# A hybrid decoder step on one core: eight dummy products in the router chain taken out

## The chip, the cores and the metric

The kernel runs on one core of one Trainium2 chip. The metric is device time in microseconds (us) of one execution. A core has five engines that run side by side and meet through semaphores: TensorE (PE, the matrix engine, whose weight loads are listed apart as PEld), VectorE (DVE), ScalarE (ACT), GpSimd (POOL) and SyncE (SP, which here only issues DMA transfers). TensorE's clock is granted at 2.4 GHz (1.00 in the profile) or at half of that (0.50).

## The reference: what is computed

One decoder layer over 264 tokens (256 of a prompt and 8 samples), all float32, model width 1024:

```
x += W_out( sigmoid(Ga h) * HGRN2(h) + sigmoid(Gb h) * MultiScalePool(h) ),  h = RMSNorm(x)
x += MoE_top4of32_clampedSwiGLU(RMSNorm(x))
x += sigmoid(RMSNorm(x) W_pg) * (p_i W_pp)
```

and a last RMSNorm. The part that matters here is the second line. A router (1024 x 32) gives each token 32 logits; the best four experts are picked, and their softmax weighs them. Each of the 32 experts has three 1024 x 1024 weight matrices (gate, up, down), some 403 MB together:

```
gate = min(xb @ w_gate[e] + b_gate[e], 7);  up = clip(xb @ w_up[e] + b_up[e], -7, 7)
act  = (up + 1) * gate * sigmoid(1.702 * gate);  y = act @ w_down[e] + b_down[e]
```

## The kernel before, in words

Every engine has one instruction stream, written out by hand in order. There is no planner: an engine does its instructions one after another and waits where `wait_ge` says so.

**Up to the router.** Projections, the recurrent mixer, the pooling mixer and W_out are computed for three token tiles (128, 128 and 8 tokens). PSUM banks are handed out by a fixed list of jobs; `fill_done` tells that TensorE has filled a bank, `drain_done` that VectorE ("v") or ScalarE ("a") has emptied it.

**The router chain** (lines 858 to 883 on TensorE, 1502 to 1566 on VectorE):
- TensorE turns the normalised rows h2 (line 587) and multiplies them by the router matrix (`logits`, line 854), tile by tile; tile 1 is the last.
- VectorE adds the bias, finds the best values and their indices (lines 1506 to 1519), makes a one-hot of them (line 1525) and the mask `msk` of chosen experts (line 1526). That last instruction raises semaphore `s_rt` to 2.
- TensorE meanwhile runs six dummy products (`keep_warm(6, bank[5])`, line 868, recorded under line 597): 128x128 identity by 128x256 of h2, into a bank that nobody reads. It then waits for `s_rt` 2 and computes the *rank* of each token within its expert (lines 873 and 876: products of a triangular matrix or ones with `msk`) and the *count* per expert (line 882). Then come two more dummies (line 884).
- VectorE turns the ranks into slot numbers (lines 1534 and 1540) and makes the first token selector `oh` (`select_tokens(0)`, line 1489).

**Between the router and the loop.** TensorE gathers the tokens of the first two experts (`gather`, line 926, and `gather_samples`, line 936), with `turn_weights` (line 892) and the bias products `down_biases` (lines 904 and 909) in between. VectorE builds the routing tables all this while, then adds the bias products to x (lines 1470 and 1572) and signals the banks free. ScalarE copies the gathered rows to SBUF (`rows_in`, line 1212).

**The expert loop** runs 16 times, each time over a pair of experts: bias products (line 986), gate and up and down products (line 970), the next pair's gather (926, 936), transposes (944, 1000), and the combination back to tokens (1010, 1014). The weights come as granules of 1 MB, 24 per pair, into a ring of 16 places. SP issues the load of granule n at line 414 once `s_used` has reached n + 1. The first 16 loads are let go by instructions far ahead of the loop (the last of them by the turning of h2), so the ring is full before the loop starts. Load 17 is let go by the product with the first granule in the loop, and so on, one load for one granule used.

**After the loop** come the per-layer-input gate (weights loaded by the same queue, line 422 and 424) and the last norm.

Gate and up products read their selector, their rows and the banks as these waits say:

```
pe.wait_ge(s_esel, i + 1)
pe.wait_ge(s_xe, 2 * i + 1)
pe.wait_ge(s_free23, i + 1)
```

Of the kernel before, what the change touches and what calls it, by code (L numbers as in the profile page):

```python
# [126 lines left out]
def build(nc, x_prompt, x_sample, p_prompt, p_sample, state_hgrn, state_pool, g_mix, w_in,  # L127
          hg_lb_logits, hg_norm, w_pool, pool_scale, w_out, g_ffn, w_router, b_router, w_gate, b_gate,
          w_up, b_up, w_down, b_down, g_ple, w_ple_gate, w_ple_proj, g_final,
          y_prompt, y_sample, new_hgrn_prompt, new_pool_prompt, new_hgrn_sample, new_pool_sample):  # L130
    jobs = bank_jobs()
    order = {name: n for n, (name, _, _) in enumerate(jobs)}
    drainer = {name: e for name, _, e in jobs}
    drain_count, before = {}, {}
    seen, last = {"a": 0, "v": 0}, {}
# [6 lines left out]
    with ExitStack() as ctx:  # L142
# [4 lines left out]
        bank = [ctx.enter_context(nc.psum_tensor(f"bank{n}", [P, HALF], F32)) for n in range(8)]  # L147
        at = [0]

        def take(floats):  # L150
            at[0] += floats
            assert at[0] <= 53200, at[0]
            return at[0] - floats

        def view(start, floats, rows=P):
            return arena[0:rows, start:start + floats]
# [11 lines left out]
        ident = view(take(P), P)  # L168
# [23 lines left out]
        def rows3(start):  # L192
            return view(start, 3 * D).rearrange("p (t d) -> p t d", t=3)
# [33 lines left out]
        h2 = rows3(OG)  # L227
# [105 lines left out]
        def fill_done(ins, name):  # L333
            ins.then_inc(filled, 1)
# [29 lines left out]
        def piece(name):  # L364
            _, t, n = name
            return job_bank(name)[:, :] if t < 2 else job_bank(name)[32 * n:32 * n + NS, 0:256]
# [204 lines left out]
        def _(pe):  # L571
# [19 lines left out]
                                ins.then_inc(s_used, 1)  # L591
                        fill_done(ins, name)

            def keep_warm(n, out):

                for _ in range(n):
                    pe.matmul(out[:, 0:256], ident, h2[:, 0, 0:256], start=True, stop=True)

            def wait_turned(tag, tiles=range(NT)):
                for t in tiles:  # L600
                    for half in range(2 if t < 2 else 1):
                        wait_drained(pe, (tag, t, half))
# [50 lines left out]
            for kind in ("f", "q"):  # L653
                for h in range(H):
# [3 lines left out]
                    for k in range(KD):  # L658
                        ins = pe.matmul(job_bank((kind, h))[:, 0:T],  # L659
                                        w_slot[c % NSLOT][:, k, (h % 4) * P:(h % 4 + 1) * P], hT[:, k, :],  # L660
                                        start=(k == 0), stop=(k == KD - 1))
# [8 lines left out]
            for a in range(2):  # L670
                for b in range(NS):
                    for j in range(4):
                        h = 2 * j + a
                        pe.matmul(bank[7][32 * j:32 * j + NS, a * P:(a + 1) * P], qm[:, h, b, :], s0[:, b, h, :],
                                  start=(b == 0), stop=(b == NS - 1))
            for h in range(H):
                ins = pe.matmul(bank[7][0:NS, 2 * P + h:2 * P + h + 1], qk_s[:, h, :], ones[:, 0:1],
                                start=True, stop=True)
# [20 lines left out]
            for t in range(2):  # L699
                for half in range(2):  # L700
                    name = ("score", t, half)
                    begin(name)
                    for j in range(4):
                        h = 4 * half + j
                        ins = pe.matmul(job_bank(name)[:, j * P:(j + 1) * P], t1[:, h, toks(t)], qh[:, h, toks(t)],
                                        start=True, stop=True)
# [36 lines left out]
            for t in range(2):  # L743
                for half in range(2):
# [3 lines left out]
                    for j in range(4):  # L748
# [3 lines left out]
                                  start=(j == 0), stop=True, skip_group_check=True)  # L752
                    wait_drained(pe, ("dS", t, half, 3))
                    for j in range(4):
                        h = 4 * half + j
                        for c in range(4):
                            n = 4 * t + c
# [29 lines left out]
            for k in range(2):  # L787
                for g in range(4):
                    ins = pe.matmul(piece(("yp", 2, g)), dT[:, 2 * g + k, toks(2)], wpool[:, g, k, :],
                                    start=(k == 0), stop=(k == 1))  # L790
                    if k == 1:
                        fill_done(ins, ("yp", 2, g))
            for t in range(2):
                for half in range(2):
                    name = ("yp", t, half)
                    begin(name)
                    for gg in range(2):
                        g = 2 * half + gg
                        for k in range(2):
                            ins = pe.matmul(job_bank(name)[lanes(t), gg * 256:(gg + 1) * 256],  # L800
                                            dT[:, 2 * g + k, toks(t)], wpool[:, g, k, :],
                                            start=(k == 0), stop=(k == 1))
# [62 lines left out]
            wait_turned("h2T", (1,))  # L865
            fill_done(logits(1), ("lg",))

            keep_warm(6, bank[5])
            pe.wait_ge(s_rt, 2)
            begin(("rank",))  # L870
            for t in range(NT):
# [8 lines left out]
            for t in range(NT):  # L880
                n = TS[t]
                ins = pe.matmul(bank[2][0:8, 0:NE], ones[0:n, 0:8], msk[0:n, t, :], start=(t == 0), stop=(t == NT - 1))
            fill_done(ins, ("count",))
            keep_warm(2, bank[5])

            def turn_weights():

                pe.wait_ge(s_rt, 3)
                begin(("wT",))
                for t in range(NT):  # L890
                    for r in range(4):
                        ins = pe.matmul(bank[3][r * NE:(r + 1) * NE, toks(t)], wdn[lanes(t), t, :],
                                        ident[lanes(t), lanes(t)], start=True, stop=True, tile_position=(0, r * NE))
                fill_done(ins, ("wT",))
# [770 lines left out]
```

## Time and profile before

| what | value |
|---|---|
| time, three runs | 1355.17, 1355.27 and 1357.8 us, median 1355.27 |
| the profiled execution's own time | 1357.17 us |
| its span in the trace | 1355.4 us |
| PE busy | 1253.1 us (92%) |
| PEld, DVE, ACT, POOL busy | 575.4, 334.2, 185.3, 66.7 us |
| mean granted TensorE clock | 0.988 |
| moved by DMA | 458.72 MB, mean 338 GB/s |

The span is from the first to the last recorded instruction; the time of the execution has 1.8 us more around it. PE's busy time includes products at either clock level and products whose result nobody uses. An engine's busy share says little about the end; what a stage is worth is read from the waits and the chain of that stage.

### The profile page before, as it was taken

The numbers are of one execution on the slowest core, as the hardware profiler recorded it, in microseconds if no ns is written. First come the engines' busy times: TensorE is split into PE (matmuls) and PEld (weight loads), VectorE is DVE, ScalarE is ACT, GpSimd is POOL, SyncE is SP. The second block draws the span as 40 slices with busy tenths as digits, with TensorE's granted clock in tenths as the row PEclk, the third lists the DMA queues.
The fourth block names the chain that finished last, engine by engine and source line by source line (L and its number), as shares of the span: only waits on it lengthen the run. The fifth ranks groups of instructions, "written<-read, shape, count | busy, mean of one in ns | idle before, by whom it ended". The sixth has DMA issues, their size and how long they took to land.

```text
span 1355.4 us, 15937 instructions
## 1 busy us (share of the span) xinstructions
PE 1253.1 (92%) x6319; PEld 575.4 (42%) x6319; DVE 334.2 (25%) x635; ACT 185.3 (14%) x359; POOL 66.7 (5%) x142
## 2 busy tenths in 40 slices
PE   6999999899999999999998999999898999999895
PEld 5764445365543433434333343433334343333342
DVE  2423335132422212122111212211121221112123
ACT  3313312212001001000000100000010000001042
POOL 7020110130000000000000000000000000000000
PEclk9999999999899999999999999999999999999988
DMA  9734251575499999999999999999999999999920
GB/s 330 257 112 155 84 216 64 188 273 189 162 423 422 421 422 422 422 422 422 422 422 422 422 422 422 422 422 422 423 422 422 422 422 422 422 422 422 419 84 32
DMA packets 79360, 458.72 MB, mean 338 GB/s; under 512 B 8553, under 2 KB 9729, under 8 KB 30176
## 3 DMA queue, kind: packets, MB, share of 16 engines
q1 hardware_dynamic: 73936, 444.66, 80.2%
q0 software_dynamic: 3888, 12.88, 3.2%
q10 hardware_dynamic: 1504, 0.75, 0.2%
q8 instruction: 21, 0.34, 0.1%
q14 instruction: 11, 0.09, 0.0%
HBM read 452.36 MB, written 6.35 MB: 338 GB/s over the span
## 4 chain that ended last, share of the span: by engine, by line
PE 68%; DMA 26%; DVE 3%; ACT 1%; issue 1%; SPq 1%; POOL 0%; DVEq 0%; ACTq 0%
PE bank L970 32%; DMA arena<-in_w_down_dram 22%; PE bank L618 10%; PE bank L821 5%; PE bank L1010 4%; PE bank L659 3%; PE bank L926 3%; DMA arena<-in_w_up_dram 2%; DMA arena<-in_w_ple_proj_dram 1%; PE bank L641 1%; PE bank L936 1%; PE bank L986 1%; PE bank L1014 1%; PE bank L587 1%; PE bank L828 1%
## 5 line engine op out<-in xcount | busy, mean ns | idle before, releaser
L970 PE MATMUL bank<-arena 128*64 128x512 f32 x3072 | 677.1, 594 | 48.0 <-DMA arena<-in_w_up_dram 31.5
L970 PEld LDWEIGHTS bank<-arena 128*64 128x64 f32 x3072 | 229.3, 137 | 480.6 <-issue 480.3
L618 PE MATMUL bank<-arena 128*128 128x512 f32 x320 | 145.5, 609 | 4.5 <-ACT arena L1060 3.0
L618 PEld LDWEIGHTS bank<-arena 128*128 128x128 f32 x320 | 60.5, 194 | 81.1 <-issue 77.7
L1607 DVE TENSOR_TENSOR arena<-bank,arena 128x512 f32<-128x512 f32 (+1 forms) x96 | 61.5, 683 | 78.0 <-PE bank L1010 77.8
L926 PEld LDWEIGHTS bank<-arena 128*128 128x128 f32 x544 | 66.7, 196 | 27.2 <-issue 27.2
L926 PE MATMUL bank<-arena 128*128 128x128 f32 x544 | 73.4, 288 | 0.0
L1591 DVE TENSOR_SCALAR arena<-bank 128x512 f32<-128x512 f32 x32 | 20.6, 687 | 200.1 <-PE bank L970 200.1
L1601 DVE COPY arena<-bank 128x512 f32<-128x512 f32 x16 | 11.1, 692 | 235.8 <-PE bank L970 235.8
L821 PE MATMUL bank<-arena 128*128 128x512 f32 x144 | 65.5, 615 | 3.2 <-issue 3.2
L1585 DVE TENSOR_SCALAR arena<-bank 128x512 f32<-128x512 f32 x32 | 20.6, 687 | 186.4 <-PE bank L970 186.4
L659 PE MATMUL bank<-arena 128*128 128x264 f32 x256 | 60.9, 403 | 3.2 <-DVE arena L1333 2.6
L1010 PE MATMUL bank<-arena 128*128 128x512 f32 x128 | 59.2, 605 | 0.0
L1221 ACT ACTIVATE arena<-arena 128x1024 f32<-128x1024 f32 x16 | 16.9, 1058 | 293.0 <-DVE arena L1585 293.0
L659 PEld LDWEIGHTS bank<-arena 128*128 128x128 f32 x256 | 50.8, 199 | 12.9 <-issue 3.0
L461 POOL DMA_DIRECT2D out_dram<-arena x3 | 1.7, 551 | 1047.2 <-DVE arena L1639 1047.2
L1223 ACT ACTIVATE arena<-bank 128x264 f32<-128x264 f32 x16 | 6.3, 392 | 289.1 <-PE bank L1000 289.1
L821 PEld LDWEIGHTS bank<-arena 128*128 128x128 f32 x144 | 28.1, 198 | 38.4 <-issue 38.3
L1225 ACT ACTIVATE arena<-bank 128x512 f32<-128x512 f32 x16 | 9.6, 598 | 236.5 <-PE bank L970 236.5
L1010 PEld LDWEIGHTS bank<-arena 128*128 128x128 f32 x128 | 23.0, 189 | 24.9 <-issue 23.0
L1269 DVE COPY arena<-bank 128x512 f32<-128x512 f32 (+3 forms) x22 | 12.3, 569 | 76.7 <-PE bank L781 42.4
L944 PE MATMUL bank<-arena 128*128 128x128 f32 x128 | 19.6, 296 | 10.3 <-DVE arena L1596 10.3
(230 smaller groups left out, 730.1 us busy)
## 6 DMA issues: line engine op xcount, KB each, us to landing
arena<-in_w_gate_dram SPq DMA_DIRECT2D x128, 1024.0 KB, 26.3
arena<-in_w_up_dram SPq DMA_DIRECT2D x128, 1024.0 KB, 26.4
arena<-in_w_down_dram SPq DMA_DIRECT2D x128, 1024.0 KB, 26.3
arena<-in_w_in_dram SPq DMA_DIRECT2D x14, 2048.0 KB, 12.1
out_dram<-arena POOLq DMA_DIRECT2D x11, 512.0 KB, 3.8
arena<-in_state_hgrn_dram POOLq DMA_DIRECT2D x8, 512.0 KB, 14.2
arena<-in_w_out_dram SPq DMA_DIRECT2D x4, 1024.0 KB, 8.1
arena<-in_w_ple_gate_dram SPq DMA_DIRECT2D x4, 1024.0 KB, 26.7
```

The lines of the kernel that those rows point to most:

```text
L587: ins = pe.transpose(job_bank(name)[:, j * n:(j + 1) * n], src[0:n, t, k * P:(k + 1) * P], ident[0:n, 0:n])
L618: ins = pe.matmul(job_bank(name)[:, :], hT[:, k, toks(t)], w[:, k, :], start=(k == 0), stop=(k == KD - 1))
L659: ins = pe.matmul(job_bank((kind, h))[:, 0:T], w_slot[c % NSLOT][:, k, (h % 4) * P:(h % 4 + 1) * P], hT[:, k, :], start=(k == 0), stop=(k ...
L821: ins = pe.matmul(job_bank(name)[:, :], src[:, k, toks(t)], weights(w, k, half), start=(k == 0), stop=(k == slices - 1))
L926: ins = pe.matmul(XG[k // 4][:, (k % 4) * P:(k % 4 + 1) * P], h2[:, t, every_other(k)], oh[:, t, :], start=(k % 4 == 0 and t == 0), stop=F ...
L944: ins = pe.transpose(out[c][:, j * P:(j + 1) * P], src[:, every_other(k)], ident)
L970: ins = pe.matmul(out[c][hp(one), :], src[:, k * P + CAP * one:k * P + CAP * one + CAP], w[one][:, j, halves(c)], start=(first and k == 0) ...
L1010: ins = pe.matmul(banks[c][:, :], comb[:, toks(t)], y_sb[:, halves(c)], start=True, stop=True)
L1221: act.activation(sig_sb, g_sb, ACT.Sigmoid, scale=ALPHA).then_inc(s_gsig, 1)
L1585: ins = dve.tensor_scalar(g_sb[:, halves(c)], bank[c][:, :], LIMIT, None, ALU.min)
L1591: ins = dve.tensor_scalar(u_sb[:, halves(c)], bank[2 + c][:, :], LIMIT, -LIMIT, ALU.min, ALU.max)
L1607: ins = dve.tensor_tensor(xs, src, xs, ALU.add)
```

## The change: the eight dummies are taken out

```diff
-            def keep_warm(n, out):
-
-                for _ in range(n):
-                    pe.matmul(out[:, 0:256], ident, h2[:, 0, 0:256], start=True, stop=True)
-
@@ TensorE, after the logits of tile 1
             fill_done(logits(1), ("lg",))
 
-            keep_warm(6, bank[5])
             pe.wait_ge(s_rt, 2)
             begin(("rank",))
@@ TensorE, after the counts
             fill_done(ins, ("count",))
-            keep_warm(2, bank[5])
-
             def turn_weights():
```

The six dummies ahead of the ranks and the two ahead of the first gather go. No wait, no transfer and no other product is changed, on any engine.

## Rows read from the trace of the kernel before

**Rows 1.** The page, 40 slices: DMA share in tenths, and GB/s.
```profile
DMA  9734251575499999999999999999999999999920
GB/s 330 257 112 155 84 216 64 188 273 189 162 423 422 421 422 422 422 422 422 422 422 422 422 422 422 422 422 422 423 422 422 422 422 422 422 422 422 419 84 32
```

**Rows 2.** DMA issues on SP: start, us, queue, line, transfer, count.
```profile
302.33 31.83 SPq L414 DMA_DIRECT2D arena<-in_w_up_dram  x8
362.77 11.49 SPq L414 DMA_DIRECT2D arena<-in_w_down_dram  x8
```

**Rows 3.** Waits of PE in the loop: total us, times, longest.
```profile
PE bank L970 <- DMA arena<-in_w_up_dram: 31.5, 24, 1.3
```

**Rows 4.** The chain that ended last, near the loop's end.
```profile
1273.78 20.23 DMA arena<-in_w_ple_proj_dram
1294.01 2.02 issue
```

**Rows 5.** The chain from the router to the loop: start, us, what, how many.
```profile
334.28 1.94 PE bank L854 x16
...
338.00 2.61 PE bank L854 x16
340.61 5.28 PE bank L597 x12
345.89 0.21 PE bank L876 x2
...
347.15 0.36 PE bank L882 x6
347.51 1.06 PE bank L597 x4
348.58 2.11 PE bank L926 x16
...
355.74 1.19 PE bank L936 x16
356.94 0.04 issue
356.98 0.61 ACT arena L1212
357.58 0.44 issue
358.02 1.14 PE bank L986 x8
```

**Rows 6.** Stretches: length, busy us of PE, PEld, DVE, ACT, POOL, PEclk, DMA, GB/s.
```profile
66.00:69.40 3.40, 3.40 (x10) 2.58 (x9) 0.25 (x1) 0.00 (x0) 0.00 (x0) 0.50 1.05 405
120.60:124.00 3.40, 3.40 (x5) 1.35 (x4) 1.03 (x4) 3.40 (x13) 0.93 (x1) 0.50 0.19 60
335.60:339.00 3.40, 2.53 (x24) 2.32 (x23) 0.80 (x2) 0.60 (x1) 0.00 (x0) 1.00 1.02 419
340.60:345.90 5.30, 5.30 (x15) 4.22 (x14) 3.14 (x17) 0.21 (x1) 0.00 (x0) 0.50 0.55 230
345.90:348.60 2.70, 2.70 (x25) 2.07 (x24) 1.29 (x5) 0.00 (x0) 0.00 (x0) 1.00 0.00 0
348.60:357.00 8.40, 8.28 (x84) 5.89 (x84) 8.04 (x24) 0.42 (x2) 0.00 (x0) 1.00 0.01 2
362.80:1290.00 927.20, 868.90 (x4304) 357.14 (x4301) 188.26 (x280) 70.02 (x96) 0.00 (x0) 1.00 1.01 421
1294.90:1301.60 6.70, 5.56 (x7) 2.50 (x8) 4.20 (x7) 4.71 (x10) 0.00 (x0) 0.50 0.04 17
```

**Rows 7.** VectorE in order of time: start, us, line, operation, [idle before].
```profile
343.17 0.81 DVE L1526 TENSOR_REDUCE arena<-arena 128x96 f32<-128x384 f32 x1
...
347.20 0.26 DVE L1534 SCALAR_TENSOR_TENSOR arena<-bank,arena 128x96 f32<-128x96 f32 x1 [3.09 <-PE bank L876]
...
347.75 0.56 DVE L1489 TENSOR_TENSOR arena<-arena 128x384 f32<-128x384 f32 x1
...
356.06 1.27 DVE L1572 TENSOR_TENSOR arena<-bank,arena 8x512 f32<-8x512 f32 x2
```

## The prediction

> **What bounds the kernel now.** I read the 40 slices of the page first. The reader is to see that from slice 12 on the DMA row stays at 9 and the traffic at 422 GB/s almost to the end, and that before it both jump about [rows 1]. The long part is therefore a steady stream of weights. The stretch table confirms it: over the 927 us from 362.8 on, the DMA engines are busy throughout (1.01) at 421 GB/s [rows 6]. TensorE is the one that waits in it: 24 waits for up granules alone, 31.5 us together [rows 3]. The chain that ended last leaves the loop through the transfer of w_ple_proj [rows 4], the tail of the same queue. So the end is the moment at which this stream starts, plus a fixed amount.
>
> The issues on SP say when it starts. Eight loads are issued in the 32 us after 302.33, and the next one comes at 362.77 [rows 2]. The ring of 16 granules is full before then, and the next load is let go when the first granule has been used. The first product of the loop, line 986, starts at 358.02 and takes 1.14 us [rows 5]; the first use ends 362.77 - 358.02 = 4.75 us after that start. So each microsecond by which the loop starts later, or by which these 4.75 us get longer, is a microsecond at the end, and the reverse. What I have to find is the new start of the loop.
>
> Third, the chain of waits from the router to the loop [rows 5], with the granted clock of its stretches [rows 6] and VectorE's instructions [rows 7]. Two facts decide. The clock is already at 0.50 when the dummies begin at 340.61, after the thin logits products (0.50 from about 339.1, since 335.6 to 339.0 is still at 1.00); it returns to 1.00 at 345.9, after 5.3 us filled by dummies without a gap. And the mask is ready at 343.17 + 0.81 = 343.98 [rows 7], but the ranks start at 345.89, because the six dummies, at half clock, are still running.
>
> **The change part by part.**
>
> *Six dummies ahead of the ranks.* Twelve records take 5.28 us, 0.44 us each. Of these 343.98 - 340.61 = 3.4 us lie beside VectorE's search for the best four; the rest, 345.89 - 344.03 = 1.86 us, is on the path. Without them the ranks start at about 344.03 (0.05 us for the semaphore, such as the 0.04 us at 356.94 [rows 5]).
>
> *The clock under the ranks.* Here the saving is paid for. Without dummies TensorE stands idle from 340.61 to 344.03, while its clock is at half. Nothing gives it back before the ranks. The ranks took 347.15 - 345.89 = 1.26 us at the full clock. How much longer is a product at half? The dummies themselves show both levels: 0.44 us a record in the row of twelve, 1.06/4 = 0.265 in the row of four, a factor of 1.66; the clocks' own ratio is 2. I take 2, because short rows of a few records carry a start and an end in them that make the ratio look smaller, and keep 1.66 as the other end. The ranks then end at 344.03 + 2.52 = 346.55 (346.1 at 1.66), 0.6 us before the old 347.15. So 1.86 us saved become 0.6.
>
> *Two dummies ahead of the gather.* The selector is ready at 347.75 + 0.56 = 348.31 [rows 7], the gather starts at 348.58 when the dummies end. They cost TensorE at most 0.27 us, and I count that as gained on TensorE's side: the gather can start 348.31 + 0.04 - 347.15 = 1.20 us after the end of the ranks.
>
> *Two chains to the loop.* VectorE's has no TensorE clock in it: from the end of the ranks it works almost without a gap (8.04 of 8.40 us from 348.6 to 357.0 [rows 6]), until its last bias additions end at 356.06 + 1.27 = 357.33 [rows 7], and the loop starts 0.69 us later. From end of ranks to loop that is 358.02 - 347.15 = 10.87 us. New: 346.55 + 10.87 = 357.42, 0.6 us earlier than before. TensorE's own: the work from the first gather to the last sample product is 356.94 - 348.58 = 8.36 us at full clock, then 0.04 and 0.61 us for ScalarE's copy and 0.04 to start. Before, it would have let the loop start at 357.62; the loop started at 358.02, so TensorE's chain had 0.4 us of slack and VectorE's was the later. (The page puts the last wait down to ScalarE, which was done 0.44 us earlier; the additions and the entry into the loop behind them fit better.)
>
> Now TensorE's chain starts at 346.55 + 1.20 = 347.75, at half clock. When does the full clock come back? Rows of before give three lengths. The stretches at 66 and at 120.6 were dense at once and lasted some 3.4 us; the dummies had it back 5.3 us after their first product; the stretch from 1294.9 lasted 6.7 us, of which TensorE was busy 5.56 [rows 6]. The gathers follow an idle place, as the dummies followed thin products, so I take 5.3: full clock at 353.05. In these 5.3 us TensorE does 2.65 us of its 8.36; the other 5.71 us end at 358.76, and the loop starts 0.69 us later, at 359.45. That is 1.43 us later than before. By the other rows: with 3.4 us at half, 347.75 + 3.4 + (8.36 - 1.7) = 357.81, loop at 358.50, +0.5; with 6.7 us, 347.75 + 6.7 + (8.36 - 3.35) = 359.46, loop at 360.15, +2.1. With the factor of 1.66 and 5.3 us (ranks end 346.1, gather from 347.3): 347.3 + 5.3 + (8.36 - 3.19) = 357.8, loop at 358.5, +0.5. The value taken is +1.4, with +0.5 and +2.1 around it. What is late next is thus TensorE's own gathers and bias products, not VectorE.
>
> *The first granule.* The 4.75 us from the loop's start to the first refill stay, if the clock is back by then. If not, they double: +4.75.
>
> *The rest.* Sixteen matmul records and their weight loads less on an engine that waits for DMA through the loop; bank 5 is read by nobody then. Nothing from that, in either direction: the 5.28 us and 1.06 us of TensorE time are on no other chain.
>
> *The sum.* -1.86 (ranks earlier) + 1.26 (ranks at half clock) gives -0.6 for the end of the ranks; -0.22 at the gather's start (348.58 to 348.35); +2.65 (half of 5.3 us lost in the gathers); -0.40 because TensorE's chain had slack. Together +1.43 us. The profiled execution, at 1357.17 us of its own (span 1355.4 and 1.8 around it), would become 1358.6. It lies 1.9 us above the median of the runs, 1355.27, and one of the three runs does too (1357.8); the difference is as large as what I am after. I put the sum on the median: 1355.27 + 1.43 = 1356.7.
>
> *A rule of the skill against this change.* In an execution in which the clock had stayed full through the logits, they would end about 0.7 us earlier, and six dummies of 0.53 us each would be done before the mask: they would then cost nothing. The trace shows no such execution. The Trainium skill (TensorE: Matmul & The Clock Gate, Why this matters for your kernels) says that idle gaps between bursts of products send the clock back to half, and its Part 1 adds that how many products run at half varies between runs of the same kernel. By that rule the new idle place of 3.4 us would itself bring a fall in such executions, and the loss would be the half-clock share of the gathers without the 1.86 us in return. No run here shows it yet; the stated spread of the three runs, 2.6 us, is at least as large as such an effect. It is priced as a rival below.
>
> **The rivals.**
>
> *A: the forecast.* The clock comes back in the middle of the gathers and bias products; +0.5 to +2.1, so 1355.8 to 1357.4, likeliest 1356.7. Chance 0.5.
>
> *B: the idle place itself brings a fall that was not there before.* An execution with full clock before would have no saving at the ranks; half clock through 5.3 us of gathers costs 2.65 less the slack of 0.4, less the 0.22 at the gather: +2.0, and with 6.7 us at half +2.7. Time 1357.3 to 1358.0. For it: stretches at half elsewhere begin after idle or thin places. Against it: in the one trace the fall came before the dummies, so this place did not need an idle TensorE. Chance 0.2.
>
> *C: clearly slower, the clock stays at half into the loop.* The mechanism is the same, the place the first granule. From 347.75 all 8.36 us take 16.72: 364.47, loop at 365.16, +7.1, and the 4.75 us of the first granule double: +11.9 in all, 1367.2. It decides from the point at which the half clock outlasts the gathers, that is over 10 us of nearly unbroken products, more than any stretch in the trace (6.7). A partial form of it, a second fall at the 1 us gap ahead of the loop (356.94 to 358.02), would cost up to 4.75 on top of the +1.4: 1361.4. Chance 0.07.
>
> *D: faster, the ranks' earlier start survives.* If the clock is back when the gathers start, or if thin products lose little at half clock, VectorE's chain decides: -0.6 with the ranks at half, -1.86 if they too ran at full. 1353.4 to 1354.7. For it: VectorE's chain was the later one, and it does not slow down. Against it: from 340.6 to 347.8 TensorE is idle or in thin products, and in the trace the clock came back only behind dummies. Chance 0.13.
>
> *E: the change reaches the end in no measurable form.* The start of the stream is shifted but the end is not, because something later than the stream sets it. Time 1355.3. Against it: 927 us without a break in the stream, and the chain through its last transfer. Chance 0.1.
>
> **How the numbers follow.** A measurement of this kernel can tell about 0.2%, 2.7 us, from no change: 1352.6 and 1358.0 are the bounds. A, D and E lie within them, B at the upper one, C above it. The median itself can fall into either group of execution times (1355.2 or 1357.5), which carries some of A and B over the upper bound. Slower: 0.07 of C, 0.06 of A and B, 0.13 together. Faster: 0.03, from the bottom of D. No measurable change: 0.84. The range from 1354.4 to 1359.2 leaves out C and the lower part of D, and holds the jump of the median between its two groups on top of A.
>
> **What would show it.** Line 597 is gone. The ranks (line 876) start about 3.4 us after the last logits product, at 344.0 if the clock falls where it fell. The granted clock is at 0.50 from before the ranks to about 353. The gather (line 926) of 16 records takes about 4 us in place of 2.11. The first product of line 986 starts at 359 to 360, and SP's first issue behind the ring comes 4.75 us later. The loop's traffic stays at 421 GB/s. The prediction is wrong if line 986 starts before 358.0, if the gathers run at 1.00, or if the start of the stream and the end move by different amounts.

## The result

| | before | after |
|---|---|---|
| median of 20 executions each | 1355.81 us | 1359.38 us |
| lowest, highest | 1352.79, 1358.34 | 1355.31, 1360.99 |
| ratio after to before | | 1.0024 (95% interval 1.0015 to 1.0033) |
| profiled execution, own time | 1357.17 | 1360.33 |
| its span | 1355.4 | 1358.6 |

The kernel without the dummies is slower by 0.24%, some 3.3 us, just over the bound of 0.2%. The two profiled executions differ by 3.2 us as well, so their traces can be compared term by term (both executions lie above their medians, by 1.4 and 1.0 us). Line numbers of after are lower: 849 is 854 of before, 870 and 867 are 876 and 873 (ranks), 918 and 928 are 926 and 936 (gathers), 978 and 962 are 986 and 970.

**Profile after.** First the chain of waits from the router to the loop (start, us, what, how many), which answers to [rows 5]:

```profile
337.89 2.65 PE bank L849 x16
...
343.08 0.81 DVE arena L1518
343.89 0.04 issue
343.94 0.64 PE bank L870 x2
...
346.28 0.23 PE bank L870 x4
...
347.90 3.75 PE bank L918 x16
...
357.15 1.19 PE bank L928 x16
358.33 0.04 issue
358.38 0.61 ACT arena L1204
358.98 0.41 issue
359.39 2.09 PE bank L978 x8
```

The reader is to see three things. The ranks start at 343.94, 0.05 us behind the mask, where before they started at 345.89. They take 346.51 - 343.94 = 2.57 us for 1.26. The first 16 records of the gather take 3.75 us for 2.11. All of the time won ahead of the ranks is lost again by 357, and 1.37 us more: the loop starts at 359.39, not 358.02.

The same stretches with the granted clock (columns as in [rows 6]):

```profile
340.60:343.90 3.30, 0.00 (x0) 0.00 (x0) 3.07 (x16) 0.21 (x1) 0.00 (x0) 0.50 0.82 345
343.90:347.90 4.00, 3.06 (x20) 2.65 (x21) 1.32 (x6) 0.00 (x0) 0.00 (x0) 0.50 0.01 4
347.90:352.60 4.70, 4.70 (x33) 4.06 (x33) 4.44 (x18) 0.00 (x0) 0.00 (x0) 0.50 0.01 3
352.80:359.30 6.50, 5.49 (x50) 3.44 (x44) 3.96 (x11) 1.31 (x3) 0.00 (x0) 1.00 0.00 0
359.60:362.90 3.30, 3.30 (x12) 0.84 (x14) 0.72 (x2) 1.16 (x1) 0.00 (x0) 0.51 0.00 0
363.10:1290.00 926.90, 868.67 (x4298) 355.83 (x4294) 188.18 (x280) 68.24 (x93) 0.00 (x0) 1.00 1.01 420
```

The clock falls before the place of the dummies, as before, but stays at half until 352.6. It is at full for 6.8 us and then falls a second time, just as the loop begins (359.4 to 362.8). In before it stayed at full from 345.9 through the whole loop [rows 6]. This second fall makes the bias products of line 978 take 2.09 us for 1.14. SP's first load behind the ring is accordingly late (start, us, queue, line, transfer; [rows 2]):

```profile
365.78 11.49 SPq L414 DMA_DIRECT2D arena<-in_w_down_dram  x8
```

That is 365.78 - 359.39 = 6.39 us behind the loop's start, against 4.75. From there on the two kernels are the same: the stream runs at 420 GB/s without a break, TensorE waits for it as long as before ([rows 3]),

```profile
PE bank L962 <- DMA arena<-in_w_up_dram: 31.4, 24, 1.3
```

and the span ends 1358.6 - 365.78 = 992.8 us behind the first refill, against 1355.4 - 362.77 = 992.6. So the 3.2 us are 1.37 (loop starts later) and 1.64 (first granule takes longer), with 0.2 left over.

VectorE's last piece of work ahead of the loop is the adding of the bias products to x, four instructions and then two. These are its lines of before and, below them, of after:

```profile
353.67 2.49 DVE L1470 TENSOR_TENSOR arena<-bank,arena 128x512 f32<-128x512 f32 x4
```

```profile
355.07 2.48 DVE L1462 TENSOR_TENSOR arena<-bank,arena 128x512 f32<-128x512 f32 x4 [2.15 <-PE bank L896]
357.47 1.27 DVE L1564 TENSOR_TENSOR arena<-bank,arena 8x512 f32<-8x512 f32 x2
```

In after VectorE stands idle for 2.15 us until TensorE's bias products (line 896) end. In before it starts the same additions at 353.67, when those products have just ended (line 904, 352.58 + 1.07 = 353.65). From the start of the bias products to the loop's first product both kernels need the same: 358.02 - 352.58 = 5.44 us and 359.39 - 353.98 = 5.41 us. The whole 1.37 us therefore arise ahead of the bias products.

### The profile page after: what moved, and what is told of

Same layout as the page of the kernel before. It is cut to its first block, busy times and chain, and to the rows that moved or that the text cites. A ratio compares the mean times of both kernels' runs of the same rounds, so it can differ in the third digit from the quotient of the medians.

```text
span 1358.6 us, 15905 instructions
## 1 busy us (share of the span) xinstructions
PE 1252.0 (92%) x6303; PEld 573.5 (42%) x6303; DVE 334.2 (25%) x635; ACT 185.0 (14%) x359; POOL 66.5 (5%) x142
## 4 chain that ended last, share of the span: by engine, by line
PE 68%; DMA 25%; DVE 3%; ACT 1%; issue 1%; SPq 1%; POOL 0%; DVEq 0%; ACTq 0%
PE bank L962 32%; DMA arena<-in_w_down_dram 22%; PE bank L613 10%; PE bank L816 5%; PE bank L1002 4%; PE bank L654 3%; PE bank L918 3%; DMA arena<-in_w_up_dram 2%; DMA arena<-in_w_ple_proj_dram 1%; PE bank L636 1%; PE bank L928 1%; PE bank L978 1%; PE bank L1006 1%; PE bank L587 1%; SPq L414 1%
```

## The experiments

Each was timed in five rounds beside the kernel before, on the same chip. Executions of one kernel spread by 2 to 8 us here, so the intervals are wide (0.1%, 1.4 us). The profiles are therefore read beside them. Where the work ahead of the router ends also moves from one execution to the next, so I give two lengths for each profile: from the end of the last logits product to the loop's first product, and on to the first refill. Half clock is what the trace grants between the logits and the first granule. A length belongs to the one execution that was profiled, and the ratio to all of them: in the twelve experiments the profiled execution lay 0.4 to 2.4 us below the kernel's median, except the first of the variant with the place ahead of the loop filled, which lay 2.2 above.

| kernel | ratio (interval) | logits to loop | loop to refill | half clock, us of the span |
|---|---|---|---|---|
| before (profiled) | 1 | 17.4 | 4.75 | 339.1 to 345.9 |
| after | 1.0024 (1.0015 to 1.0033) | 18.9 | 6.4 | 338.9 to 352.6, 359.4 to 362.8 |
| after, again | 1.0035 (1.0023 to 1.0048) | 19.0 | 6.4 | 339.3 to 352.9, 359.7 to 363.1 |
| only the six out | 1.0020 (1.0010 to 1.0030) | 18.1 | 6.45 | 338.0 to 348.2, 358.5 to 361.9 |
| only the two out | 1.0006 (0.9995 to 1.0017) | 18.8 | 6.3 | 337.8 to 344.7, 348.1 to 351.5, 358.3 to 361.7 |
| three in place of six | 1.0022 (1.0011 to 1.0034) | 19.4 | 6.2 | 338.4 to 352.1, 358.9 to 362.3 |
| twelve thin ones in place of six | 1.0016 (1.0005 to 1.0028) | 19.7 | 4.7 | 336.8 to 350.5 |
| after, place ahead of the loop filled | 0.9997 (0.9989 to 1.0006) | 19.2 | 4.7 | 339.4 to 353.1 |
| the same, again | 1.0005 (0.9993 to 1.0017) | 19.2 | 4.7 | 337.1 to 350.7 |
| before, that place filled | 0.9992 (0.9981 to 1.0004) | 16.4 | 4.7 | 337.3 to 340.7 |
| before, logits filled | 0.9990 (0.9979 to 1.0002) | 17.1 | 4.7 | 345.4 to 348.8 |
| before, ahead of and behind the loop filled | 0.9990 (0.9982 to 0.9999) | 16.5 | 4.7 | 337.9 to 341.4 |
| before, all three filled | 0.9991 (0.9982 to 1.0000) | 17.4 | 4.7 | 343.5 to 346.9 |
| all three filled, the eight out | 1.0011 (1.0001 to 1.0021) | 19.7 | 4.7 | 341.1 to 351.3 |

**Only the six out.**

```diff
-            keep_warm(6, bank[5])
```

> Only the six dummies ahead of the ranks go; the two ahead of the first gather stay. Clock theory (the loss is half-clock work: +1.4 us until the loop starts, +1.6 us in the first granule): the ranks start at 344.0 at half clock, the two dummies run at half clock (some 1.8 us instead of 1.06) and hold the gather back until about 348.6; the clock comes back no later than with all eight out (352.7), so the loop starts at 358.5 to 360. Time +1 to +4 us against the kernel before, close to the kernel after. Rival (the two dummies ahead of the gather were what kept the clock up, the six only cost): the time is that of the kernel before or 0.6 to 1.9 us less, with the loop at 356.2 to 357.4.

Measured: 1.0020, about what the whole change costs. The rival is out: the two dummies alone don't bring the time back. They do run at half clock (2.01 us for four records). The clock is back 9.2 us behind the logits, where the kernel after needed 12.1, and the loop starts 0.8 us sooner behind them. The second fall comes all the same.

**Only the two out.**

```diff
-            keep_warm(2, bank[5])
```

> Only the two dummies ahead of the first gather go; the six stay. Clock theory: the clock is back at 345.9 as before, the gather starts 0.2 to 0.3 us earlier, and VectorE's chain (10.87 us from the end of the ranks to the loop) hides that: the loop starts at 358.0, time within 0.5 us of the kernel before. Rival (the idle place of about 1 us behind the counts brings a fall): half clock in the gathers, +1.5 to +3 us.

Measured: 1.0006, an interval that takes in both no change and 0.17%. The profiled execution speaks for the rival, though: with the clock back at 344.7, TensorE idles behind the counts, and the clock falls again as the gathers begin (length, busy us by engine, PEclk, DMA, GB/s):

```profile
344.80:348.00 3.20, 2.14 (x25) 1.89 (x24) 1.74 (x7) 0.00 (x0) 0.00 (x0) 1.00 0.00 0
348.20:351.40 3.20, 3.20 (x28) 2.82 (x27) 3.01 (x13) 0.00 (x0) 0.00 (x0) 0.50 0.02 5
```

TensorE is busy for 2.14 of 3.20 us, and thinly, then at half for the gathers. In this execution the missing two cost 1.4 us up to the loop. How often that happens is not settled by 12 executions.

**Three in place of six.**

```diff
-            keep_warm(6, bank[5])
+            keep_warm(3, bank[5])
```

> Three dummies ahead of the ranks in place of six; the two ahead of the gather stay. At half clock three take 2.6 us and end at 343.3, before the mask (344.0), so the ranks start as early as with none. Clock theory: the full clock comes back later than with six (345.9), at some point between 346 and 352.7; with it the loop starts at 357.4 to 359.4, time between the kernel before and the kernel after. Rival (three are enough to bring the clock back at 345.9): the loop starts at 356.7 to 357.4, time 0.6 to 1.3 us under the kernel before.

Measured: 1.0022, as bad as none. The ranks started with the mask and the time that this won was lost again: half clock until 352.1. The clock theory's place for the return holds (346 to 352.7), at its late end, and the loop starts at 359.26. The rival is out. So it can't be had both ways in this place: with six the ranks wait and get the full clock, with three they start on time at half.

**Twelve thin ones in place of the six.**

```diff
-            keep_warm(6, bank[5])
+            for _ in range(12):
+                pe.matmul(bank[5][:, 0:NE], ident, h2[:, 0, 0:NE], start=True, stop=True)
-            keep_warm(2, bank[5])
```

> The six dummies become twelve thin ones (128x128 identity by 128x32), which take about as long at half clock (24 records of 0.22 us, 5.2 us) and move an eighth of the columns each; the two others go. If what counts is how much the dummies stream (as after the thin logits products, where the clock fell): the clock stays at half as in the kernel after, and on top the ranks start as late as before, 345.9, so the loop starts at 360.5 to 361.5, time +4 to +5.5 us. If it only counts that TensorE is never idle: the clock is back at 345.9 and the time is that of the kernel before.

TensorE is never idle from the logits to the ranks here; the stretches of this kernel, then the chain:

```profile
336.90:350.40 13.50, 12.60 (x66) 12.18 (x66) 7.21 (x31) 0.21 (x1) 0.00 (x0) 0.50 0.32 134
338.50:343.60 5.10, 5.10 (x25) 5.10 (x26) 3.14 (x17) 0.21 (x1) 0.00 (x0) 0.50 0.54 222
```

```profile
338.49 5.12 PE bank L869 x24
343.61 0.43 PE bank L877 x2
...
347.37 3.50 PE bank L926 x16
```

Measured: 1.0016, slower than before, and the clock stays at half for 13.7 us although TensorE is busy for 12.6 of 13.5. The two kinds of filling keep the engine equally busy and take equally long. Behind the thin ones the clock did not rise in this profile. With the six wide ones it rose in all four profiles in which it had fallen before them, by the time they ended or sooner (345.9, 344.7, 340.7 and 341.4; they ended at 345.89, 344.85, 342.25 and 342.80). The size expected, +4 to +5.5 us, was too large: measured is +2.2. In this execution no second fall came ahead of the loop, which the expectation had counted in.

**The kernel after with the place ahead of the loop filled.** The place is the 1.06 us between the last sample product and the loop.

```diff
-            keep_warm(6, bank[5])
-            keep_warm(2, bank[5])
+            wait_drained(pe, ("bd", 0, 1))
+            keep_warm(3, bank[5])
             for name in [("count",), ("bd", 0, 1), ("bd", 1, 1), ("bd2", 0), ("bd2", 1)]:
```

> The kernel after, with three dummies (1.3 us at full clock) in the idle place of 1.06 us between the last sample product and the loop. Clock theory: the half-clock stretch over the gathers stays (339 to 352.7, loop at 359.4 to 359.7), but the second one, 359.5 to 362.9, is gone, so the first granule is used 4.75 us after the loop's start and not 6.4; time 1.3 to 1.6 us under the kernel after, some 1.6 to 2 us over the kernel before. Rival (the second fall comes from the lean stretch as a whole, not from the idle place): it stays, and the time is that of the kernel after or 0.2 us more.

> The kernel without the eight dummies but with three in the idle place ahead of the loop, once more. Measured before at 0.9997 of the kernel before (0.9989 to 1.0006), which would mean that this place was the whole loss. The profiles say otherwise: the loop started 19.2 us after the last logits product against 17.4 before, so half clock in the gathers is still paid (1.4 us or so) and only the part in the first granule is saved. By them 1.0005 to 1.0015 is due; if the place was the whole loss, 0.9990 to 1.0003.

The second fall is gone in both profiles. The chain of the first one:

```profile
357.78 1.14 PE bank L934 x16
358.92 1.49 PE bank L597 x6
...
360.42 1.07 PE bank L984 x8
```

with the clock in those stretches:

```profile
339.50:353.00 13.50, 9.18 (x61) 8.30 (x60) 8.52 (x38) 0.21 (x1) 0.00 (x0) 0.50 0.34 144
353.20:360.40 7.20, 7.20 (x66) 4.73 (x62) 4.72 (x13) 1.76 (x4) 0.00 (x0) 1.00 0.00 0
360.50:365.00 4.50, 4.50 (x26) 1.46 (x28) 0.56 (x1) 0.90 (x1) 0.00 (x0) 1.00 0.00 0
```

The bias products take 1.07 us and the refill comes 4.7 us behind the loop's start, as in before, though the long half-clock stretch over the gathers is still there. So the 1.6 us in the first granule belong to this idle place; of them 0.3 us are spent again, because the loop starts that much later behind the logits (19.2 us for 18.9). The times say more than that: 0.9997 and 1.0005 against 1.0024 and 1.0035, differences of 0.27 and 0.30%, where 1.6 us are 0.12%. From the half widths of the intervals I estimate these differences to be uncertain by 0.12 and 0.17%, so 0.12% lies just outside both, and the 1.6 to 2 us over the kernel before that were expected did not come. What the rest of the gain is, no run shows.

**The kernel after, again**, beside the last two kernels below.

> The kernel after once more, on the chip of the two fillings beside it. Clock theory: as measured, 0.15 to 0.33% over the kernel before. In its profiled execution the clock is at half over the ranks and part of the gathers; where it comes back may differ by some us, and a half-clock stretch at the start of the loop may be there or not. If the difference of 3.2 us was a chance of the chips it ran on, it falls within 0.05% here.

Measured: 1.0035 (1.0023 to 1.0048), from 6 executions. The loss is no chance of the chips. The second profile has the same two half-clock stretches, 0.3 us later.

**The kernel before with the same place filled.**

```diff
+            wait_drained(pe, ("bd", 0, 1))
+            keep_warm(3, bank[5])
```

> The kernel before, with three dummies in the idle place of 1.06 us ahead of the loop; its eight dummies stay. Clock theory: executions of the kernel before in which a half-clock stretch begins at this place (1.6 us or more lost in the first granule) lose it no more; those like the profiled one, at full clock there, gain nothing and may lose 0.2 us because three dummies take 1.3 us. Time 0.5 to 1.5 us under the kernel before, and so also under the variant with this filling and without the eight by 1 to 2 us (that one still has the half-clock gathers). Rival (only one of the two fillings is needed, the eight dummies add nothing once the gap is filled): the same time as that variant, within 0.5 us.

Measured: 0.9992, up to 1.0004: not told apart from before, nor from the variant without the eight. In its profile the clock was back at 340.7, so about half of the six dummies ran at full clock, and from there to the first granule TensorE was busy without a gap (147 records):

```profile
340.80:359.30 18.50, 18.50 (x147) 11.91 (x147) 11.78 (x37) 2.76 (x4) 0.00 (x0) 1.00 0.04 15
```

**The kernel before with the logits' idle places filled.**

```diff
+                if t == 0:
+                    keep_warm(1, bank[5])
                 wait_turned("h2T", (t,))
                 logits(t)
             turn_rows("h2T", h2, h2_ready, tiles=(1,))
+            keep_warm(2, bank[5])
```

> The kernel before, with one dummy in the idle place of 0.47 us and two in that of 0.87 us between the turning of h2 and the logits, at full clock (0.43 us each). Clock theory: the fall at 339.1 comes from the lean logits stretch; if these three dummies prevent it, the six dummies behind the logits run at full clock, end by 342.6, before the mask at 343.3, and the ranks start when the mask is there: the loop starts some 2.5 us earlier (0.6 from the last logits at full clock, 1.86 from the ranks), time 2 to 2.5 us under the kernel before. Rival (the thin logits products bring the fall, filled or not): the fall stays, the time is that of the kernel before within 0.5 us.

Measured: 0.9990 (0.9979 to 1.0002). In the profiled execution the fall at 339 is gone and the six dummies run at full clock, but another fall comes 6 us later, under the two dummies ahead of the gathers, and lasts through most of the first gather:

```profile
330.00:345.30 15.30, 14.54 (x132) 11.90 (x131) 8.29 (x28) 3.74 (x7) 0.00 (x0) 1.00 0.68 276
345.50:348.70 3.20, 3.20 (x15) 3.02 (x15) 2.96 (x10) 0.00 (x0) 0.00 (x0) 0.50 0.02 5
```

Both theories were half right: the fall can be moved, and a good part of the gain goes with the next one.

**The kernel before with the places ahead of and behind the loop filled.**

```diff
                     pair(PER * q, n)
+            pe.wait_ge(s_free45, PAIRS + 1)
+            keep_warm(6, bank[5])
             more = pe.value_load(flag)
```

> The kernel before, with the three dummies ahead of the loop and six more (2.6 us at full clock) in the idle place of 3.2 us behind the loop (1292.8 to 1296.0), ahead of the products with w_ple_proj. Clock theory: the half-clock stretch from 1294.9 to 1301.6 goes or shrinks, which gives back 1.4 to 2.8 us there, on top of the 0.5 to 1.5 us ahead of the loop: time 2 to 4 us under the kernel before. Rival (behind the loop VectorE and ScalarE set the time, not TensorE's clock): the time of the variant with the filling ahead of the loop alone.

Measured: 0.9990 (0.9982 to 0.9999). This profile has no half-clock stretch behind the loop, where [rows 6] has one of 6.7 us:

```profile
1290.00:1300.00 10.00, 8.53 (x26) 4.79 (x27) 5.63 (x10) 5.43 (x12) 0.00 (x0) 1.00 0.19 75
```

That the filling pays is not shown. On the same chip the variant with the place ahead of the loop filled alone has 0.9992, and the mean of its executions is the same within 0.1 us (1354.72 against 1354.70), which is what the rival expected. The traces say why. In the eleven profiles without this filling the stretch behind the loop lasted 6.8 us in two, 3.4 in seven, and was absent in two (only the two out; three in place of six). From the first refill to the end they took 992.6 and 992.8 us, 991.1 to 991.9, and 989.9 and 990.1. The three profiles with the filling have no such stretch and took 991.0 to 991.6, longer than the two without stretch and without filling. In before the next products come 3.19 us behind the loop's last ones:

```profile
1296.04 9.89 PE L821 MATMUL bank<-arena 128*128 128x512 f32 x16 [3.19 <-issue]
```

With the six dummies in between they come 4.5 to 4.9 us behind them. These 16 records then take 7.1 us at full clock, for 9.9 here and 8.6 to 8.8 with a stretch of 3.4 us. So the filling gives back 1.5 to 2.8 us when the clock would have fallen and costs 1.3 to 1.8 us each time.

**All three filled, with and without the eight.** The first has the edits of the three fillings above on the kernel before. The second has these as well:

```diff
-            keep_warm(6, bank[5])
-            keep_warm(2, bank[5])
```

> The kernel before with its eight dummies and all three fillings: three dummies in the logits' idle places, three ahead of the loop, six behind it. Clock theory: the gains of the three places are of different stretches and add up: 0.5 to 1.5 (ahead of the loop), 0.5 to 2 (logits), 0.5 to 1.5 us (behind the loop), time 1.5 to 4 us under the kernel before, lower than each filling by itself. Rival (a fall that is kept from one place comes at the next one and costs as much there): no lower than 1.3 us under the kernel before, as the fillings by themselves.

> The same three fillings, without the eight dummies of the change. Against the kernel with all fillings it is the change once more, with the second fall ahead of the loop prevented. Clock theory: the idle place of 3.4 us behind the logits is still there, at full or half clock, and brings or keeps half clock over the ranks and part of the gathers: the loop starts 0.5 to 2 us later behind the last logits product, time 0.7 to 2 us over the kernel with all fillings. Rival (the eight are of no use once the other places are filled, and only hold the ranks back): the same time or up to 1 us less.

These two ran on the same chip and differ by the change alone: 0.9991 with the eight, 1.0011 without, medians 1354.41 and 1357.83 us. In the two profiles the way from the end of the logits to the first refill is 22.1 and 24.3 us long. So the change costs about 0.2% also where the place ahead of the loop is filled and the logits leave the clock at full. Without the eight the clock, at 1.00 until 341, falls in the new idle place itself and stays down for 10.2 us:

```profile
331.00:341.00 10.00, 7.15 (x83) 6.18 (x80) 6.00 (x22) 3.34 (x7) 0.00 (x0) 1.00 1.00 392
341.20:351.20 10.00, 8.73 (x63) 7.65 (x64) 6.37 (x25) 0.39 (x1) 0.00 (x0) 0.50 0.05 20
```

This is the mechanism of rival B of the prediction, seen in a trace, and the 2.2 us between the two profiles are within the 2.0 to 2.7 us that B was priced at. With all fillings and the eight, on the other hand, the time is no better than with two of the fillings (0.9991 and 0.9990): the gains don't add up.

## Why the prediction was right, and where not

The direction and the mechanism (half clock over the ranks and gathers) were right. The range ended at 1359.2 and the median is 1359.38; over 20 executions before itself came out 0.5 us above the three that the sum started from. The sum, +1.4 us, is less than half of the +3.3 measured.

- *The start of the stream sets the end.* Right for the two profiled executions: refill to end 992.6 and 992.8 us. It is not a constant of the kernel: the second profile of after has its refill 3.04 us later than before, but its span is only 1.5 us longer, since its half-clock stretch behind the loop lasted 3.4 us and not 6.8.
- *Ranks start with the mask.* Forecast 344.03, measured 343.94.
- *The ranks at half clock.* Forecast 2.52 us, measured 2.57; the factor of 2 and not 1.66.
- *The loop starts at 359.45.* Measured 359.39, +1.37 for +1.43. This nearness is in part luck, since three terms were off and cancel. The half clock in the gathers was put at +2.65; from the first gather to the bias products after needs 353.98 - 347.90 = 6.08 us for 352.58 - 348.58 = 4.00, so +2.08. The slack of 0.40 us that TensorE's chain was to have gave nothing. VectorE's chain, read as free of TensorE's clock, waits for the bias products, so it moves with them. This was hidden in before, where VectorE was ready only 0.05 us ahead of them (353.60 against 353.65). Whether the loop waits for VectorE's additions or for ScalarE's copy isn't settled by these two traces: it starts 0.69 and 0.65 us behind the one, 0.44 and 0.41 behind the other. And the gather's start gave 0.04 us and not 0.22: it comes 0.25 us behind the selector in after, where two dummies are missing, and 0.27 in before. The measured terms are -0.64 - 0.04 + 2.08 - 0.03 = +1.37.
- *The gathers at half clock until about 353.* Forecast 353.05, read off the 5.3 us that the dummies had needed; measured 352.6. That was nearer than the reasoning deserves: the other kernels have it back at 348.2, 350.5, 352.1 and 353.1.
- *The first granule.* This is the step that failed. "The 4.75 us from the loop's start to the first refill stay, if the clock is back by then." It was back, at 352.6, and fell again at the end of the 1.06 us without products ahead of the loop. Measured 6.39 us, so +1.64 that the sum had at nothing. The prediction had this only as the partial form of rival C, at up to 4.75 us and a small chance. None of the six profiles with this place filled has a fall there, and five of the eight with it unfilled have. The kernel before had the place too, at full clock in its profile; five of the six profiles with all or some of the eight missing and the place unfilled have the fall, the one with thin fillers has not.
- *The two dummies ahead of the gather.* I booked them as a gain of 0.22 us. With them out the one profile has a fall of its own (348.1 to 351.5) and the time is 1.0006, so the gain is not to be seen and a loss of 0.17% not excluded.
- *The chances.* 0.84 for no measurable change was too much. The sum of +1.4 us was one term short, and the term left out had the same cause as the others, so it should have been expected along with them. In the spread of the 20 executions rivals A, B and the partial C are mixed; how often each comes can't be read from one profile per kernel.

## What to carry to other kernels

Dummy products can be worth their time where a lean stretch (thin products, waits of a us or so) is followed by TensorE work that is on the path. Here the eight were worth 0.2 to 0.35%, though the six of them held the ranks back by 1.9 us in the profile of before. When work is taken out, price not only the stretch behind it at half clock but every further idle place that follows until TensorE is dense again. Before an engine's chain is called free of the clock, look whether it was only just ahead of a product that it waits for, as VectorE was by 0.05 us. And try the fill on the chip: thin products in place of wide ones, three in place of six, or six behind the loop gave nothing here.

## What the runs showed of the hardware

- Twelve fillers with 32 columns each kept TensorE busy for 5.1 of 5.1 us, and the granted clock stayed at 0.50 throughout and for 7 us more. PE's busy time doesn't tell its clock.
- The same code, at the same place, had its clock back after 3.4 us in one execution (337.3 to 340.7) and after 6.8 in another (339.1 to 345.9), both with six dummies behind the logits and no change ahead of them. The clock's moves are not fixed to the program. The 20 executions of one kernel spread over 5.6 us; how much of this the clock makes up isn't shown.
- Behind the loop eleven profiles with the same code there have a half-clock stretch of 6.8 us (two), of 3.4 us (seven) or none (two).
- A fall that one filling prevents can come later in the same chain: at 339 before, at 345.4 with the logits filled, at 343.5 with all three places filled.
